# Two transformer blocks with 64 experts on one core: expert loops with sixteen blocks per turn, and the last output pass by column halves

## The chip, the core and the metric

The kernel runs on one core of a Trainium2 chip. The metric is the time of one execution on the device, in microseconds. Runs of the kernel before are 1090.98 to 1095.73 us, with a median of 1094.42 of three.

## The reference

256 tokens of 1024 features go through two layers. The first has three kinds of attention (block-wise, dilated, sliding window with sinks) with gated branches and an output projection. The second has a modulation by a condition, a short convolution beside a sparse attention, and then a mixture of experts. Only the last matters here:

```python
def moe(h, w_router, router_bias, w1, w3, w2, ws1, ws3, ws2):
    scores = sigmoid(t @ w_router)
    _, eidx = top_k(scores + router_bias, 8)              # 8 of 64 experts for each token
    g = take(scores, eidx); g = g / sum(g) * 2.5
    # (token, expert) pairs are sorted by expert and padded to blocks of 128 rows
    out = for each block: swiglu(t[toks], w1[e], w3[e], w2[e]) * gs[:, None]
    routed = segment_sum(out, row_tok)
    shared = swiglu(t, ws1, ws3, ws2)
    return routed + shared
x = x + gate2 * moe(h2, ...)
```

An expert has 1024 x 256 weights twice and 256 x 1024 once, 3 MB in float32. How many blocks have work depends on the data: at least one for each expert in use, at most 79. With these inputs there are 33.

## The kernel before

Each of the five engines has its own instruction stream, and semaphores join them. Up to about 685 us of the span the streams are straight: an order that the program works out while it is built. Then comes the expert part, where the number of blocks `n_work` is known only at run time. Each engine there has a `Fori` loop. A turn of it holds four blocks written one after the other (`BODY = 4`), since buffers rotate over four or two places and semaphore names hang on the block's number modulo 4. A turn is inside an `If` on the whole turn, and each block in it inside an `If` of its own. The number of turns is fixed when the program is built, for the most blocks that can be: 20 on each engine (19 on SP, whose first four blocks stand ahead). Where there are fewer blocks, the engine goes through the turns that are left and does nothing in them.

One block of TensorE (`expert_block`, L2018 to L2047) is 24 up matmuls (L2020, weights and rows each split into a rounded part and a rest, three products), the turning of the next block's gathered rows (L1997), the put of the block before into the four sum banks (`scatter`, L2005, four matmuls for each half of the columns), the turning of the hidden rows (L2035), the search for the tokens of the block after next (L1987), and 12 down matmuls (L2047). The first block stands apart ahead of the loop, so the loop holds blocks 1 to 78, 1 to 32 with these data.

One block of VectorE (L1643 to L1665) is the rests of the down weights (L1646), the rests of the next up weights (L1619), the product of the two hidden halves (L1651), the rests of the next rows (L1613), the rest of the hidden rows (L1654), two small ones on tokens and gates (L1605, L1606), more up weights, and `y_lo` for each half of the columns (L1663). ScalarE makes the rounded parts beside it. VectorE has no block apart. SP loads the weights of a block when the place is free (`down_lo`), GpSimd makes the pick and put matrices and gathers rows.

The end: after the loop TensorE runs 22 matmuls of ones into an unused bank (`keep_busy(("last_put",))`), then the put of the last block, eight matmuls over both halves of the columns and both groups of 128 tokens, and a one-column matmul that tells VectorE (`experts_summed`). VectorE multiplies each of four pieces of 128 x 512 by the gate (L1672) and adds it to `x` (L1675), and SP stores 128 tokens of 1024 columns when two pieces are there (L785):

```python
            for t in range(NT):
                sp.wait_ge(S("out_ready"), 2 * t + 2)
                sp.dma_start(out[0, t * P:(t + 1) * P, :], x[:, t, :]).then_inc(S("out_stored"), 16)
```

## Time and profile before

| What | us |
|---|---|
| median of three runs | 1094.42 |
| lowest and highest run | 1090.98, 1095.73 |
| the profiled execution, its own time | 1096.29 |
| its span, first to last instruction | 1094.5 |
| TensorE busy in the span | 1032.3 |
| VectorE busy in the span | 796.3 |
| ScalarE busy in the span | 585.7 |
| GpSimd busy in the span | 219.9 |

Busy time is the sum of an engine's instructions; branches, register and semaphore instructions are not counted. "Idle before" names what released an engine; "issue" is time in which it waited for nothing that the profile shows. The clock is that granted to TensorE, as a share of its full speed. The queues named "instruction" carry the program itself. The profiled execution is 1.8 us longer than its span and 1.9 us longer than the median.

### The profile page before, as it was taken

To read this page: it belongs to the slowest core of one execution; us is meant where nothing else is said; L and a number is where in the kernel's file an instruction comes from. 1 tells how busy PE (TensorE), PEld (TensorE's weight loads), DVE (VectorE), ACT (ScalarE), POOL (GpSimd) and SP (SyncE) were. 2 spreads that over 40 slices of the span, in tenths; PEclk is the share of its full clock that TensorE was granted. 3 is DMA by queue.
4 is the path that set the end of the run, shared out by engine and by line. 5 is a ranking of instruction groups with operands and counts; after the bars stand their busy time and mean duration, and the time that the engine had idled before them with its cause. 6 is when DMAs were issued, how large, how long until landed. Compare 5 with 4: busy or idle time off the path is not lost. (4 is left out here: it accounts for less than half of the span.)

```text
span 1094.5 us, 16677 instructions
## 1 busy us (share of the span) xinstructions
PE 1032.3 (94%) x5226; PEld 834.4 (76%) x5226; DVE 796.3 (73%) x1324; ACT 585.7 (54%) x895; POOL 219.9 (20%) x237
## 2 busy tenths in 40 slices
PE   8999999997999999998979899999999999999994
PEld 7778878786776676786769787778888888888883
DVE  4677887676754443556696554998999999999993
ACT  4455554433434332434344242777777777777771
POOL 4142220001000000041130001332423323323320
PEclk9999999998999899998999899999999999999998
DMA  9876766748525243435233215988888888888871
GB/s 317 276 266 220 268 237 212 233 163 284 193 96 173 92 154 116 165 94 214 89 107 126 77 59 210 348 304 326 338 310 331 341 306 335 334 309 344 333 287 57
DMA packets 91206, 247.40 MB, mean 226 GB/s; under 512 B 13244, under 2 KB 23925, under 8 KB 77842
## 3 DMA queue, kind: packets, MB, share of 16 engines
q1 hardware_dynamic: 84578, 226.36, 57.6%
q0 software_dynamic: 6000, 19.96, 4.8%
q8 instruction: 29, 0.48, 0.2%
q10 hardware_dynamic: 576, 0.41, 0.1%
q14 instruction: 23, 0.19, 0.0%
HBM read 244.27 MB, written 2.29 MB: 225 GB/s over the span
## 5 line engine op out<-in xcount | busy, mean ns | idle before, releaser
L1766 PE MATMUL bank<-w_hi,a_hi 128*128 128x512 f32 (+2 forms) x512 | 208.1, 406 | 11.2 <-DVE w_lo L1229 5.5
L1766 PE MATMUL bank<-w_lo,a_hi 128*128 128x512 f32 (+2 forms) x512 | 198.8, 388 | 0.0
L1766 PE MATMUL bank<-w_hi,a_lo 128*128 128x512 f32 (+2 forms) x512 | 198.7, 388 | 0.0
L1229 DVE TENSOR_TENSOR w_lo<-ring,w_hi 128x1024 fp32r<-128x1024 f32 (+2 forms) x134 | 154.7, 1179 | 51.2 <-ACT w_hi L952 46.8
L952 ACT ACTIVATE w_hi<-ring 128x1024 fp32r<-128x1024 f32 (+2 forms) x140 | 141.4, 1024 | 89.2 <-PE bank L1766 85.8
L1619 DVE TENSOR_TENSOR up_lo<-raw_weights,up_hi 128x1024 fp32r<-128x1024 f32 x136 | 164.2, 1248 | 3.0
L1112 ACT ACTIVATE up_hi<-raw_weights 128x1024 fp32r<-128x1024 f32 x136 | 135.8, 1050 | 0.0
L1766 PEld LDWEIGHTS bank<-w_hi,a_hi 128*128 128x128 f32 x512 | 98.0, 191 | 42.1 <-issue 20.1
L798 POOL TENSOR_SCALAR mean_squares<-mean_squares 128x8 f32<-128x8 f32 (+2 forms) x32 | 9.7, 302 | 549.8 <-ACT logits L905 294.7
L1766 PEld LDWEIGHTS bank<-w_hi,a_lo 128*128 128x128 f32 x512 | 98.1, 192 | 20.3
L1766 PEld LDWEIGHTS bank<-w_lo,a_hi 128*128 128x128 f32 x512 | 98.3, 192 | 18.6 <-issue 1.4
L2020 PE MATMUL bank<-up_hi,x_block_hi 128*128 128x512 f32 x264 | 104.3, 395 | 1.2 <-issue 1.2
L2020 PE MATMUL bank<-up_hi,x_block_lo 128*128 128x512 f32 x264 | 104.5, 396 | 0.0
L2020 PE MATMUL bank<-up_lo,x_block_hi 128*128 128x512 f32 x264 | 104.3, 395 | 0.0
L892 POOL TENSOR_SCALAR put<-block_rows,consts 128x256 fp32r<-128x256 f32 x33 | 39.7, 1203 | 242.4 <-PE bank L2005 128.1
L1646 DVE TENSOR_TENSOR down_lo<-raw_weights,down_hi 128x1024 fp32r<-128x1024 f32 x66 | 78.6, 1231 | 7.0 <-ACT down_hi L1129 7.0
L1382 DVE SCALAR_TENSOR_TENSOR ada_acc<-merged,c_col,ada_acc 128x512 f32<-128x512 f32 x84 | 62.8, 748 | 19.4 <-DMA merged<-in_w_ada_dram 16.7
L1129 ACT ACTIVATE down_hi<-raw_weights 128x1024 fp32r<-128x1024 f32 x66 | 66.0, 1050 | 0.3 <-issue 0.3
L1148 ACT ACTIVATE y_hi<-bank,block_gates 128x512 fp32r<-128x512 f32 x66 | 45.5, 689 | 31.3 <-PE bank L2047 31.3
L2020 PEld LDWEIGHTS bank<-up_hi,x_block_hi 128*128 128x128 f32 x264 | 49.6, 188 | 13.2 <-issue 1.4
L2020 PEld LDWEIGHTS bank<-up_lo,x_block_hi 128*128 128x128 f32 x264 | 49.6, 188 | 11.9
L2020 PEld LDWEIGHTS bank<-up_hi,x_block_lo 128*128 128x128 f32 x264 | 49.6, 188 | 11.8
(260 smaller groups left out, 1906.9 us busy)
## 6 DMA issues: line engine op xcount, KB each, us to landing
raw_weights<-in_w_dram SPq DMA_DIRECT2D x102, 1024.0 KB, 7.0
ring<-in_w_in_dram SPq DMA_DIRECT2D x58, 1024.0 KB, 5.3
merged<-in_w_ada_dram SPq DMA_DIRECT2D x96, 256.0 KB, 5.3
ring<-in_w_out_dram SPq DMA_DIRECT2D x8, 1024.0 KB, 5.4
ring<-in_w_branch_dram SPq DMA_DIRECT2D x6, 1024.0 KB, 5.0
bias<-rel_rows SPq DMA_DIRECT2D x40, 128.0 KB, 5.1
block_rows<-place_rows SPq DMA_DIRECT2D x34, 128.0 KB, 8.7
ring<-in_ws_dram SPq DMA_DIRECT2D x2, 1024.0 KB, 5.3
```

What stands on the lines that cost most here:

```text
L798: gp.tensor_scalar(msum[:, z, 0:width], msum[:, z, 0:width], 1.0 / count, EPS, ALU.mult, ALU.add)\
L892: gp.tensor_scalar(put[:, :], row4[:, r, :], consts[:, C_COL:C_COL + 1], None, ALU.is_equal)\
L952: act.activation(w_parts[0][:, 2 * p:2 * p + 2, 0:w], view(j, kind)[:, 2 * p:2 * p + 2, :], ACT.Copy)\
L1112: act.activation(up_hi[:, r % 2, 4 * kh:4 * kh + 4, m, :], raw_up(raw[:, 1 - r % 2, :], kh, m), ACT.Copy)\
L1129: act.activation(down_hi[:, f, :], raw[:, 1 - r % 2][:, UP + f * DM:UP + (f + 1) * DM], ACT.Copy)\
L1148: act.activation(y_hi[:, hf * CH:(hf + 1) * CH], y_b[hf][:, :], ACT.Copy, scale=gcol[:, r, 0:1])\
L1229: dve.tensor_tensor(w_parts[1][:, 2 * p:2 * p + 2, 0:w], view(JOB[it[1:3]], kind)[:, 2 * p:2 * p + 2, :], w_parts[0][:, 2 * p:2 * p + 2, 0 ...
L1382: dve.scalar_tensor_tensor(out=o, in0=ada_row(q), scalar=c_col[:, 1, k:k + 1], in1=o, op0=ALU.mult, op1=ALU.add) .then_inc(S("ada_step" if ...
L1619: dve.tensor_tensor(up_lo[:, r % 2, 4 * kh:4 * kh + 4, m, :], raw_up(raw[:, 1 - r % 2, :], kh, m), up_hi[:, r % 2, 4 * kh:4 * kh + 4, m, : ...
L1646: dve.tensor_tensor(down_lo[:, f, :], raw[:, 1 - r % 2][:, UP + f * DM:UP + (f + 1) * DM], down_hi[:, f, :].bitcast(F32), ALU.subtract).th ...
L1766: mm = pe.matmul(ps[:, 0:wide], a_parts[za][:, k, t * P:(t + 1) * P], w_parts[zw][:, k, 0:wide], start=start, stop=stop)
L2020: mm = pe.matmul(hidden_b[:, :], (xe_hi, xe_lo)[zx][:, k, :], (up_hi, up_lo)[zw][:, r % 2, k].rearrange("p m n -> p (m n)"), start=(k == 0 ...
```

## The change

`LONG` is 16. The loops of TensorE and VectorE get sixteen blocks in a turn, so 5 turns on each; the block's body stays as it was, and is a function on VectorE now. VectorE's first block stands ahead of its loop, as TensorE's did. The loops of ScalarE, GpSimd and SP are not changed. The 22 matmuls of ones and the one-column matmul are removed, and the last put of each half of the columns tells VectorE itself. VectorE works by halves: the two products of a half, then its two sums; SP stores each of the four pieces by itself.

```diff
--- before.py
+++ after.py
@@ -372,9 +372,10 @@
 KEEP_BUSY = {("start",): 16, ("half", "proj", 2, 0): 9, ("proj", 2, 0): 4, ("flip", 15, 2): 5,
              ("turn_branch", 2): 6, ("xturn", 1, 0): 4, ("xturn", 1, 1): 15, ("proj2", 0, 0): 4, ("turn2", 0, 3, 0): 7,
              ("turn2", 1): 10, ("value", 31): 8, ("turn_branch", 3, 1): 17, ("out2", 0, 0): 4, ("route", 0): 4,
-             ("route", 1): 5, ("ranks",): 7, ("tokens", 0): 5, ("last_put",): 22}
+             ("route", 1): 5, ("ranks",): 7, ("tokens", 0): 5}
 
 BODY = 4
+LONG = 4 * BODY
 UP, DOWN = 2 * KT * ED, FT * DM
 N_SMALL = 15
 N_LATE = 6
@@ -780,10 +781,12 @@
                         sp.wait_ge(S("down_lo"), 2 * i - 2)
                         load_down(r, load_up(i, r))
                         load_places(i, r)
-            for t in range(NT):
-                sp.wait_ge(S("out_ready"), 2 * t + 2)
-                sp.dma_start(out[0, t * P:(t + 1) * P, :], x[:, t, :]).then_inc(S("out_stored"), 16)
-            sp.wait_ge(S("out_stored"), 16 * NT)
+            for hf in range(2):
+                c = slice(hf * CH, hf * CH + CH)
+                for t in range(NT):
+                    sp.wait_ge(S("out_ready"), 2 * hf + t + 1)
+                    sp.dma_start(out[0, t * P:(t + 1) * P, c], x[:, t, c]).then_inc(S("out_stored"), 16)
+            sp.wait_ge(S("out_stored"), 16 * 2 * NT)
 
 
         @block.gpsimd
@@ -1636,43 +1639,50 @@
             rest_of_rows(0)
             dve.wait_ge(S("work_ready"), 2)
             n_work = dve.value_load(work[0:1, 0:1], min_val=0, max_val=MAX_WORK)
-            with dve.Fori(0, -(-MAX_WORK // BODY)) as m4, dve.If(n_work > m4 * BODY):
-                for r in range(BODY):
-                    i = m4 * BODY + r
+            def expert_block(i, r):
+
+                nxt = (r + 1) % BODY
+                for f in range(FT):
+                    dve.wait_ge(S("down_hi"), 2 * i + f + 1)
+                    dve.tensor_tensor(down_lo[:, f, :], raw[:, 1 - r % 2][:, UP + f * DM:UP + (f + 1) * DM],
+                                      down_hi[:, f, :].bitcast(F32), ALU.subtract).then_inc(S("down_lo"), 1)
+                for m in range(2):
+                    rest_of_up_weights(i + 1, nxt, 0, m)
+                dve.wait_ge(S("silu_done"), i + 1)
+                dve.tensor_tensor(he, hs[:, 0, :], hidden_b[:, ED:2 * ED], ALU.mult).then_inc(S("h_done"), 1)
+                rest_of_rows(i + 1)
+                dve.wait_ge(S("h_hi_ready"), i + 1)
+                dve.tensor_tensor(h_lo[:, :, :], turned_b[:, 0:ED].rearrange("p (f n) -> p f n", f=FT),
+                                  h_hi[:, :, :].bitcast(F32), ALU.subtract).then_inc(S("h_lo_ready"), 1)
+                take_tokens(i + 2, (r + 2) % BODY)
+                for m in range(2):
+                    rest_of_up_weights(i + 1, nxt, 1, m)
+                for hf in range(2):
+
+                    dve.wait_ge(S(f"y_hi_{hf}"), i + 1)
+                    c = slice(hf * CH, (hf + 1) * CH)
+                    dve.scalar_tensor_tensor(out=y_lo[:, c], in0=y_b[hf][:, :], scalar=gcol[:, r, 0:1],
+                                             in1=y_hi[:, c].bitcast(F32), op0=ALU.mult, op1=ALU.subtract)\
+                       .then_inc(S(f"y_lo_{hf}"), 1)
+
+            expert_block(0, 0)
+            with dve.Fori(0, -(-(MAX_WORK - 1) // LONG)) as turn, dve.If(n_work > turn * LONG + 1):
+                for b in range(LONG):
+                    i = turn * LONG + (b + 1)
                     with dve.If(n_work > i):
-                        nxt = (r + 1) % BODY
-                        for f in range(FT):
-                            dve.wait_ge(S("down_hi"), 2 * i + f + 1)
-                            dve.tensor_tensor(down_lo[:, f, :], raw[:, 1 - r % 2][:, UP + f * DM:UP + (f + 1) * DM],
-                                              down_hi[:, f, :].bitcast(F32), ALU.subtract).then_inc(S("down_lo"), 1)
-                        for m in range(2):
-                            rest_of_up_weights(i + 1, nxt, 0, m)
-                        dve.wait_ge(S("silu_done"), i + 1)
-                        dve.tensor_tensor(he, hs[:, 0, :], hidden_b[:, ED:2 * ED], ALU.mult).then_inc(S("h_done"), 1)
-                        rest_of_rows(i + 1)
-                        dve.wait_ge(S("h_hi_ready"), i + 1)
-                        dve.tensor_tensor(h_lo[:, :, :], turned_b[:, 0:ED].rearrange("p (f n) -> p f n", f=FT),
-                                          h_hi[:, :, :].bitcast(F32), ALU.subtract).then_inc(S("h_lo_ready"), 1)
-                        take_tokens(i + 2, (r + 2) % BODY)
-                        for m in range(2):
-                            rest_of_up_weights(i + 1, nxt, 1, m)
-                        for hf in range(2):
-
-                            dve.wait_ge(S(f"y_hi_{hf}"), i + 1)
-                            c = slice(hf * CH, (hf + 1) * CH)
-                            dve.scalar_tensor_tensor(out=y_lo[:, c], in0=y_b[hf][:, :], scalar=gcol[:, r, 0:1],
-                                                     in1=y_hi[:, c].bitcast(F32), op0=ALU.mult, op1=ALU.subtract)\
-                               .then_inc(S(f"y_lo_{hf}"), 1)
-
-            dve.wait_ge(S("experts_summed"), 1)
-            for t in range(NT):
-                for hf in range(2):
-                    tmp = qn[:, hf, :]
-                    o = x[:, t, hf * CH:hf * CH + CH]
-                    dve.tensor_tensor(tmp, acc_b[2 * t + hf][:, :], gate_bc[:, 1, hf * CH:hf * CH + CH], ALU.mult)\
+                        expert_block(i, (b + 1) % BODY)
+
+            for hf in range(2):
+                c = slice(hf * CH, hf * CH + CH)
+                dve.wait_ge(S("experts_summed"), hf + 1)
+                for t in range(NT):
+                    if hf:
+                        dve.wait_ge(S("out_ready"), t + 1)
+                    dve.tensor_tensor(qn[:, t, :], acc_b[2 * t + hf][:, :], gate_bc[:, 1, c], ALU.mult)\
                        .then_inc(S("final_step"), 1)
-                    dve.wait_ge(S("final_step"), 2 * t + hf + 1)
-                    dve.tensor_tensor(o, o, tmp, ALU.add).then_inc(S("out_ready"), 1)
+                for t in range(NT):
+                    dve.wait_ge(S("final_step"), 2 * hf + t + 1)
+                    dve.tensor_tensor(x[:, t, c], x[:, t, c], qn[:, t, :], ALU.add).then_inc(S("out_ready"), 1)
 
 
         @block.tensor
@@ -2071,18 +2081,14 @@
             mm.then_inc(S("block_done"), 1)
             turn_rows(0, 1)
             expert_block(0, 0, 1)
-            with pe.Fori(0, -(-(MAX_WORK - 1) // BODY)) as m4, pe.If(n_work > m4 * BODY + 1):
-                for b in range(BODY):
-                    i = m4 * BODY + (b + 1)
+            with pe.Fori(0, -(-(MAX_WORK - 1) // LONG)) as turn, pe.If(n_work > turn * LONG + 1):
+                for b in range(LONG):
+                    i = turn * LONG + (b + 1)
                     with pe.If(n_work > i):
-                        expert_block(i, (b + 1) % BODY, m4 + 1 + (b + 2) // BODY)
-            keep_busy(("last_put",), turned_b)
+                        expert_block(i, (b + 1) % BODY, turn * (LONG // BODY) + (1 + (b + 2) // BODY))
             pe.wait_ge(S("put_ready"), n_work)
             for hf in range(2):
-                mm = scatter(hf, n_work)
-            mm.then_inc(S("block_done"), 1)
-
-            pe.matmul(y_b[0][0:1, 0:1], ones[:, 0:1], ones[:, 0:1], start=True, stop=True).then_inc(S("experts_summed"), 1)
+                scatter(hf, n_work).then_inc(S("experts_summed"), 1)
 
 
 
```

In the built program, TensorE's stream behind the last block of its loop, before (`bank` stands for the sum banks and the unused one, `ones` for the filling):

```order
L2074 COMPARE_AND_BRANCH
L1706 MATMUL bank<-ones 128x128 x22
L2005 MATMUL bank<-y_hi,put 128x512 [waits y_lo_0,put_ready]
L2005 MATMUL bank<-y_lo,put 128x512
L2005 MATMUL bank<-y_hi,put 128x512
L2005 MATMUL bank<-y_lo,put 128x512
L2005 MATMUL bank<-y_hi,put 128x512 [waits y_lo_1]
L2005 MATMUL bank<-y_lo,put 128x512
L2005 MATMUL bank<-y_hi,put 128x512
L2005 MATMUL bank<-y_lo,put 128x512
L2085 MATMUL bank<-ones 1x1
L389 UNCONDITIONAL_BRANCH
```

and now:

```order
L2084 COMPARE_AND_BRANCH
L2015 MATMUL bank<-y_hi,put 128x512 [waits y_lo_0,put_ready]
L2015 MATMUL bank<-y_lo,put 128x512
L2015 MATMUL bank<-y_hi,put 128x512
L2015 MATMUL bank<-y_lo,put 128x512
L2015 MATMUL bank<-y_hi,put 128x512 [waits y_lo_1]
L2015 MATMUL bank<-y_lo,put 128x512
L2015 MATMUL bank<-y_hi,put 128x512
L2015 MATMUL bank<-y_lo,put 128x512
L390 UNCONDITIONAL_BRANCH
```

The filling matmuls and the one-column matmul between the loop and VectorE are gone, and the eight puts follow the loop's branch.

VectorE's stream behind its loop, before (`qn` is the temporary, L1672 the product with the gate, L1675 the sum):

```order
L1639 COMPARE_AND_BRANCH
L1672 TENSOR_TENSOR qn<-bank,gate_bc 128x512 [waits experts_summed]
L1675 TENSOR_TENSOR x<-x,qn 128x512 [waits final_step]
L1672 TENSOR_TENSOR qn<-bank,gate_bc 128x512
L1675 TENSOR_TENSOR x<-x,qn 128x512 [waits final_step]
L1672 TENSOR_TENSOR qn<-bank,gate_bc 128x512
L1675 TENSOR_TENSOR x<-x,qn 128x512 [waits final_step]
L1672 TENSOR_TENSOR qn<-bank,gate_bc 128x512
L1675 TENSOR_TENSOR x<-x,qn 128x512 [waits final_step]
L389 UNCONDITIONAL_BRANCH
```

and now (L1681 the product, L1685 the sum):

```order
L1669 COMPARE_AND_BRANCH
L1681 TENSOR_TENSOR qn<-bank,gate_bc 128x512 [waits experts_summed]
L1681 TENSOR_TENSOR qn<-bank,gate_bc 128x512
L1685 TENSOR_TENSOR x<-x,qn 128x512 [waits final_step] x2
L1681 TENSOR_TENSOR qn<-bank,gate_bc 128x512 [waits out_ready,experts_summed]
L1681 TENSOR_TENSOR qn<-bank,gate_bc 128x512 [waits out_ready]
L1685 TENSOR_TENSOR x<-x,qn 128x512 [waits final_step] x2
L390 UNCONDITIONAL_BRANCH
```

Products and sums alternated behind one signal; now two products stand ahead of two sums, once for each half.

## Rows read from the trace of the kernel before

**Rows 1.** The page: busy time, share of the span and instructions of each engine.
```profile
PE 1032.3 (94%) x5226; PEld 834.4 (76%) x5226; DVE 796.3 (73%) x1324; ACT 585.7 (54%) x895; POOL 219.9 (20%) x237
```

**Rows 2.** Stretches, one per TensorE turn: us, busy time of each engine, clock, DMA.
```profile
697.25:744.87 47.62, 46.67 (x226) 38.09 (x224) 43.56 (x58) 35.77 (x48) 17.89 (x18) 1.00 0.85 322
...
977.68:1024.02 46.34, 46.34 (x225) 38.04 (x224) 43.29 (x58) 35.73 (x48) 15.25 (x17) 1.00 0.87 330
```

**Rows 3.** Waits of TensorE, 697.25 to 1070.8: us in total, times, longest.
```profile
PE bank L1997 <- DMA x_gathered<-h_rows,block_tokens: 1.1, 3, 0.5
```

**Rows 4.** Chain that ended last: start us, us, what.
```profile
1021.30 2.88 PE bank L2047 x12
1024.18 5.59 PE bank L2020 x24
...
1032.99 2.89 PE bank L2047 x12
1035.88 5.60 PE bank L2020 x24
...
1070.71 6.27 issue
```

**Rows 5.** Timeline of TensorE: start us, us, instruction, idle before it.
```profile
1066.39 0.39 PE L2035 MATMUL bank<-consts,hT 128*128 128x128 f32 x2
...
1070.08 0.62 PE L2047 MATMUL bank<-down_hi,h_lo 128*128 128x512 f32 x2
1076.98 7.02 PE L1706 MATMUL bank<-ones 128*128 128x128 f32 x44 [6.27 <-issue]
1083.75 0.47 PE L2005 MATMUL bank<-y_hi,put 128*128 128x512 f32 x1
...
1085.78 0.19 PE L2085 MATMUL bank<-ones 128*1 128x1 f32 x2
```

**Rows 6.** Timeline of VectorE over the last block and the end.
```profile
1060.73 2.42 DVE L1646 TENSOR_TENSOR down_lo<-raw_weights,down_hi 128x1024 fp32r<-128x1024 f32 x2 [0.23 <-ACT down_hi L1129]
...
1065.35 0.41 DVE L1651 TENSOR_TENSOR hT<-hs,bank 128x256 f32<-128x256 f32 x1
...
1071.46 0.75 DVE L1663 SCALAR_TENSOR_TENSOR y_lo<-bank,block_gates,y_hi 128x512 fp32r<-128x512 f32 x1 [0.21 <-ACT y_hi L1148]
1086.01 0.69 DVE L1672 TENSOR_TENSOR qn<-bank,gate_bc 128x512 f32<-128x512 f32 x1 [13.79 <-PE bank L2085]
...
1090.71 0.69 DVE L1675 TENSOR_TENSOR x<-x,qn 128x512 f32<-128x512 f32 x1
```

**Rows 7.** Stretches behind the last down matmul; columns as in rows 2.
```profile
1070.80:1073.90 3.10, 0.00 (x0) 0.00 (x0) 1.20 (x2) 0.63 (x1) 0.00 (x0) 1.00 0.59 169
1074.10:1080.60 6.50, 3.62 (x17) 3.63 (x18) 0.00 (x0) 0.00 (x0) 0.00 (x0) 0.50 0.00 0
1081.00:1083.70 2.70, 2.70 (x26) 2.70 (x26) 0.00 (x0) 0.00 (x0) 0.00 (x0) 1.00 0.00 0
```

**Rows 8.** Line L785, SP's stores: ns min/median/max to issue one.
```profile
L785 SPq DMA_DIRECT2D out_dram<-x x2: 343/355/367, 1088.8 to 1091.4; - x2
```

**Rows 9.** DMA issues, whole span: KB each, median us to landing.
```profile
out_dram<-x SPq DMA_DIRECT2D x2, 512.0 KB, 2.6
...
block_rows<-place_rows SPq DMA_DIRECT2D x34, 128.0 KB, 8.7
...
place_rows<-prow SPq DMA_DIRECT2D x1, 128.0 KB, 1.7
```

**Rows 10.** DMA queues, 742 to 744, the instruction queue: packets, MB, share.
```profile
q14 instruction: 1, 0.01, 1.0%
```

**Rows 11.** DMA queues, 745 to 1071, all there are.
```profile
q1 hardware_dynamic: 19851, 89.60, 72.4%
q0 software_dynamic: 4032, 14.68, 11.2%
```

**Rows 12.** DMA queues, 734 to 736, the other instruction queue.
```profile
q8 instruction: 1, 0.02, 3.3%
```

## The prediction

> **What bounds the kernel now.** I read four views in this order: the page's busy times, the stretches by turn of the expert loop, the chain that ended last, and the timeline after the last block.
>
> TensorE is busy 94% of the span, VectorE 73% [rows 1]. In the expert loop TensorE has no slack: eight turns of four blocks take 46.3 to 47.6 us, of which it works 46.3 to 46.7 [rows 2], 11.6 us a block. VectorE works 43.2 to 43.6 us of the same stretches, so it is nearly full too, with some 0.8 us free per block. All that TensorE waits for in these 373 us is the gathered rows, 1.1 us [rows 3]. Going from one turn to the next is not seen: the chain has the down matmuls ending at 1024.18 and the next up matmuls starting there, where a turn of TensorE ends, just as at 1035.88 inside a turn [rows 4].
>
> The end is different. The last down matmul ends at 1070.71; TensorE then does nothing for 6.27 us, with "issue" as its reason, runs the 44 pieces of its 22 filling matmuls for 7.02 us, and only at 1083.75 starts the last puts, although VectorE had finished what they need at 1072.21 [rows 5, 6]. The 6.27 us stand where the loop goes through its empty turns: it is written for up to 79 blocks, 33 are there, and the eight turns of work are followed by twelve in which the outer test fails, 0.52 us each. After the puts come eight VectorE operations, 1086.01 to 1091.40, and 3.1 us until the span ends.
>
> **The change part by part.**
>
> *Empty turns on TensorE.* The loop has 5 turns, 2 in use and 3 empty. At 0.52 us they cost 1.57 in place of 6.27: the puts can start at 1072.28, just behind VectorE's 1072.21. I take 0.52 although TensorE's sequencer may have run ahead of the matmuls, which would make a turn a little dearer and start it a little earlier; both ways the end stays near 1072. The Trainium skill, in Advanced Engine Details and Errata, Control Flow Timing, gives 108 ns for a compare-and-branch, and an empty turn has two. By that, twelve would take 2.6 us and nine fewer would save 1.9 us. The trace has 6.27 us for them, so the trace's price stands.
>
> *Filling matmuls.* They go: minus 7.02 us [rows 5]. They were there for the clock. It is at 1.00 until 1073.9 and at 0.50 from 1074.1 to 1080.6 [rows 7]: it fell some 3.3 us after TensorE stopped. If TensorE stops for 0.7 to 3 us only, the puts run at 1.00. At 0.50 a piece of filling takes 0.20 us instead of 0.10 (3.63 us for 18, 2.70 for 26), so the four puts ahead of VectorE would cost 0.9 us more. I take nothing and keep 0.9 for the range.
>
> *Signals by half.* The last matmul of each column half now tells VectorE, so it starts after four puts, not eight and the one-column matmul. Before, 1083.75 to 1086.01 is 2.26 us; now 4 x 0.233 and the delay of some 0.3 make 1.25: minus 1.0.
>
> *Sums and stores.* VectorE's eight operations are the same in shape and number, reordered: two products, two sums, per half. At 5.39 us for eight [rows 6] they cost the same. The new waits on `out_ready` protect the temporary; they name an operation at least two before, so nothing is added. The second half's signal comes 0.93 us after the first, inside the first four operations. SP now issues four stores instead of two, 0.36 us each [rows 8], and the last starts behind the last sum as before. It carries 256 KB instead of 512: two of 512 KB took 2.6 us to land [rows 9], with the data part about half of it, so minus 0.6.
>
> *Sum if nothing else happens:* the puts start at 1072.28, VectorE at 1073.5, ends at 1078.9, and 2.5 us later, at 1081.4, the span ends: minus 13.1.
>
> *Fewer back edges.* TensorE has one between blocks in place of seven, VectorE one (after block 16) in place of eight. By the chain each is worth nothing while the code is at hand [rows 4].
>
> *Longer loops.* This is where I see a cost. A block is 56 matmuls with as many weight loads and some 13 other instructions; the loop's body on TensorE grows from about 500 to 2000 instructions, on VectorE from 100 to 400. Before, the last instruction packet is on the wire between 742 and 744 [rows 10]; from 745 to 1071 only the two data queues move anything [rows 11]. So the whole short loop stayed at hand. Whether the long one does, no row shows. If it does not, the way back needs a fetch. Its price from below: one 16 KB packet takes 3.3% of 2 us of 16 engines, 1.1 us [rows 12]; a small transfer in a quiet stretch, the 128 KB of `place_rows`, lands after 1.7 us, and the stores after 2.6. From above: 128 KB under the loop's load take 8.7 us [rows 9], but those stand behind megabytes in their own queue, and instructions have a queue of their own. I take 3 us inside the loop and 2 to 2.6 at the end, nearer to the packet and the quiet transfers, and keep 1.1 and 8.7 for the range.
>
> In the middle, VectorE's fetch starts when its last y_lo is under way: 0.75 us of that, the 0.2 us it waits for `down_hi` anyway, and the 0.6 us between its product for the hidden rows (done 1065.76) and the transpose of it (1066.39) [rows 5, 6] hide 1.6 of the 3. TensorE loses 1.4 us, and its own fetch lies behind the queued down matmuls and beside that: 1.5 in all. At the end VectorE's loop leaves after 1072.2 + 2.3 + 3 x 0.52 = 1076.1; it starts 2.6 us later than in the sum above. TensorE's own 2.3 us put its start at 1074.6 and its first half at 1075.8, ahead of that. So 13.1 - 1.5 - 2.6 = 9.0 us are left.
>
> **Which of the two?** The Trainium skill, in Runtime: NRT & Kernel Launch, Instruction fetch mechanics, says that a taken branch to a target outside a window of two pages forces a fetch before execution goes on. With it already the short loop of TensorE, 500 instructions long, would fetch on its jumps, and the trace shows none [rows 11]. The page also has 2048 instructions for TensorE and 512 for the others; by that the long bodies fit barely, if what is fetched ahead pushes nothing out. My choice is a judgement: what keeps 500 instructions at hand need not keep 2000, and on VectorE 400 need not stay where 100 did; that one of the two has lost its head by the end of a turn is a little likelier than not.
>
> **The rivals.**
>
> *A. Everything stays at hand.* Then the sum above: minus 13.1, 1081.3. For it: the short loop kept all of its code. Against it: nothing of this length has been tried in the trace. 32%.
>
> *B. One fetch, but under load at the price of loaded transfers [rows 9].* VectorE's way back after block 16 waits up to 8.7 us, 7.1 of them seen by TensorE: 13.1 - 7.1 - 2.6 = 3.4 saved, 1091.0. Against it: an instruction packet has its own queue. 8%.
>
> *C. Every jump between the loop's head and its end fetches.* The three empty turns on VectorE then cost two fetches each: its last operations start at 1072.2 + 6p + 1.57, and with the middle p - 1.6 the span ends at 1080.1 + 7p. At p = 2 that is 1094.1, no change; it is slower than before by over 0.5% from p = 2.9 on, 1101 at 3. For it: head and end are 2000 instructions apart. Against it: once head and end have both been fetched, nothing in an empty turn needs a third place. 8%.
>
> *D. The turns never were the 6.27 us,* and TensorE waited for something unseen. Then that idle time stays, the filling matmuls go, and 13.1 - 4.7 = 8.4 are saved, 1086.0. Against it: all that the puts need was there at 1072.21. 4%, and it lies in the forecast's range.
>
> **How the numbers follow.** The profiled execution took 1096.29 us with a span of 1094.5; the median of the runs is 1094.42, and the savings are taken off that. The forecast (one fetch on each way back) has 48%: 1094.4 - 9.0 = 1085.4, by itself 1083 to 1089. The range reaches down to A with its own spread, and up to a dearer fetch: 1080.5 to 1090. It leaves out most of B and C. A measurement tells 0.5%, 5.5 us, from no change: faster is below 1088.9, slower above 1099.9. Faster: the forecast's 46, A's 32, D's 4 and a little of B, 0.85; slower: C above 2.9 us a fetch, 0.05; the rest, 0.10, is within.
>
> **What would show it.** In the changed profile: no filling matmuls after the last down matmul; TensorE idle there for 1.5 us (A) or 3.5 to 4.5 (forecast); VectorE's first final product within 1.3 us of the first put (A) or held up 1 to 2 us more by its own loop; instruction packets on their queues still at the end of the span and around block 16 to 17 (forecast), none there (A), several among the empty turns (C). Around block 17 one stretch of TensorE longer by 1 to 2 us. The puts at clock 1.00, 0.23 us apart. The eight last operations in 5.4 us. I am wrong if the gap after the last down matmul stays at 6 us, if the loop's 373 us grow by over 4, or if the end after VectorE's last sum is not shorter.

## The result, and the profile after

The changed kernel is slower: 1105.18 us median (1099.62 to 1107.52), the kernel before 1093.43 (1090.98 to 1095.73), ratio 1.0092 with a 95% interval of 1.0068 to 1.0117. The profiled execution took 1099.62 us with a span of 1097.8, so it is the quickest of its runs; its span is 3.3 us longer than the 1094.5 of before. The accounts below are of the two profiled executions, and most of the 11.75 us between the medians is not in them (see "what stays open").

The 3.3 us of span are the sum of a loop that lost and an end that gained. From the start of the second block to the start of the last, before took 361.6 us (697.25 to 1058.83), the changed kernel 374.75 (697.17 to 1071.92): +13.2. From the last down matmul to the end, before took 23.8 us (1070.71 to 1094.5), now 14.2 (1083.64 to 1097.8): -9.6. The start and the last block together give -0.3.

**The loop.** The waits of TensorE from the second block to the last down matmul (us in total, times, longest), where [rows 3] had 1.1 us, 3 times:

```profile
PE bank L2007 <- DMA x_gathered<-h_rows,block_tokens: 6.8, 11, 1.2
PE bank L2030 <- issue: 4.1, 1, 4.1
```

The second line is the one way back. It stands in the timeline of TensorE between block 16 and block 17 (start, us, instruction, idle before it):

```profile
887.72 0.63 PE L2057 MATMUL bank<-down_hi,h_lo 128*128 128x512 f32 x2
892.41 0.49 PE L2030 MATMUL bank<-up_hi,x_block_hi 128*128 128x512 f32 x1 [4.07 <-issue]
...
893.36 0.63 PE L2030 MATMUL bank<-up_hi,x_block_hi 128*128 128x512 f32 x1
893.78 0.63 PE L2030 MATMUL bank<-up_lo,x_block_hi 128*128 128x512 f32 x1
...
896.34 0.44 PE L2030 MATMUL bank<-up_lo,x_block_hi 128*128 128x512 f32 x1
896.62 0.40 PE L2030 MATMUL bank<-up_hi,x_block_lo 128*128 128x512 f32 x1
```

and in that of VectorE, at its own way back:

```profile
895.10 2.36 DVE L1647 TENSOR_TENSOR down_lo<-raw_weights,down_hi 128x1024 fp32r<-128x1024 f32 x2 [5.24 <-issue]
```

The idle 4.07 us are not all of TensorE's fetch. The duration of its jumps (PEldq is the sequencer that feeds TensorE; count, ns min/median/max, first and last start) gives it whole:

```profile
L2084 PEldq COMPARE_BRANCH  x2: 75/3120/6165, 885.5 to 891.9; - x2
```

The sequencer runs ahead of the matmuls. It took the jump back at 885.5 and held it for 6.17 us, and the down matmuls already issued kept TensorE busy for the first 2.9 of them, until 888.35. The rest and a few instructions ahead of the first matmul are the 4.07. One packet of q14, at 892.8, lies in VectorE's idle time; the next, at 895.4, came when VectorE was at work again.

After the 4.07 us the matmuls stand 0.43 us apart instead of 0.23 until 896.3: the clock had dropped. The windows show it (columns as in [rows 2]): the granted clock is 1.00 during the rest and 0.50, its lower level, once TensorE is back.

```profile
888.40:892.30 3.90, 0.00 (x0) 0.00 (x0) 1.25 (x2) 3.90 (x5) 0.91 (x2) 1.00 0.98 381
...
893.30:896.30 3.00, 3.00 (x8) 2.34 (x7) 1.20 (x2) 0.00 (x0) 0.00 (x0) 0.50 0.07 22
```

Block 16 with the way back took 15.78 us, block 17 13.21, against some 11.6: 5.8 us for one turn.

The rest of the 13.2 us are the late gathers. Outside those two blocks, 11 blocks took more than 12.1 us, 8.8 us over 11.6 in all; before, two did (12.18 and 12.32). What is new in the profile is the instruction queues. From 745 on, before had only data queues moving [rows 11]; the changed kernel, 697 to 1058:

```profile
q8 instruction: 15, 0.25, 0.3%
q14 instruction: 10, 0.08, 0.1%
```

q8 brings 16 KB at a time to TensorE (experiments 6 and 7 tell the queues apart), one packet for about every second block: eight for a turn of sixteen. Their times here are to 0.5 us. Apart from those of the way back, 14 packets of q8 lie in the loop. Each of the 11 long blocks had one on the wire while its gathered rows were: the rows are asked for 1.6 us before the block starts and needed 5.6 us after, and the packets were at 710.5, 734.5, 758.5, 784, 817.5, 839.5, 865, 908.5, 931.5, 955.5 and 1060, with those blocks starting at 708.7, 732.7, 756.5, 780.2, 816.3, 840.2, 864.1, 905.6, 929.5, 953.3 and 1059.5. No block without one was over 12.1 us. The landings say the same. In the changed kernel the gathers that were issued 10.0 to 10.3 us into a block, with a packet of q8 starting 1 to 4 us behind the issue, took 7.7 to 7.9 us to land (seven of them; an eighth, with two packets in its flight at the way back, took 8.8). Before, the twenty issued 10.0 to 10.5 us into a block with no packet took 6.5 to 7.4, with a median of 6.95.

**The end.** TensorE, in place of [rows 5]:

```profile
1083.01 0.63 PE L2057 MATMUL bank<-down_hi,h_lo 128*128 128x512 f32 x2
1088.10 0.77 PE L2015 MATMUL bank<-y_hi,put 128*128 128x512 f32 x1 [4.46 <-issue]
1088.66 0.63 PE L2015 MATMUL bank<-y_lo,put 128*128 128x512 f32 x1
1089.09 0.63 PE L2015 MATMUL bank<-y_hi,put 128*128 128x512 f32 x1
```

VectorE, in place of [rows 6]:

```profile
1084.40 0.75 DVE L1664 SCALAR_TENSOR_TENSOR y_lo<-bank,block_gates,y_hi 128x512 fp32r<-128x512 f32 x1 [0.21 <-ACT y_hi L1151]
1090.37 1.29 DVE L1681 TENSOR_TENSOR qn<-bank,gate_bc 128x512 f32<-128x512 f32 x2 [5.22 <-PE bank L2015]
1091.58 1.28 DVE L1685 TENSOR_TENSOR x<-x,qn 128x512 f32<-128x512 f32 x2
```

The 5.22 us are put down to the puts, but the chain that ended last goes through VectorE's own jumps (DVEq is its sequencer; start, us, what):

```profile
1084.48 0.06 DVEq L1669
1084.55 3.68 issue
1088.22 0.06 DVEq L1669
...
1088.39 0.28 issue
1088.68 0.04 DVEq L1669
...
1088.81 0.23 issue
1089.04 0.06 DVEq L1669
...
1090.37 1.29 DVE qn L1681 x2
```

That is one fetch of 3.68 us and then six pairs of records some 0.4 us apart, two for a turn: three empty turns of 0.7 us. TensorE's jumps at the end:

```profile
L2084 PEldq COMPARE_BRANCH  x7: 83/221/4902, 1080.8 to 1087.8; - x7
```

Its fetch took 4.90 us from 1080.8, 2.9 of them behind the last down matmuls, and three empty turns of some 0.7 us followed. The instruction queues, 1081 to 1097.8, move again:

```profile
q8 instruction: 3, 0.05, 1.5%
q14 instruction: 3, 0.02, 0.5%
```

### The profile page after: what moved, and what is told of

Same layout as the page of the kernel before. It is cut to its first block and busy times, and to the rows that moved or that the text cites. A ratio compares the mean times of both kernels' runs of the same rounds, so it can differ in the third digit from the quotient of the medians.

```text
span 1097.8 us, 16465 instructions
## 1 busy us (share of the span) xinstructions
PE 1028.8 (94%) x5180; PEld 829.0 (76%) x5180; DVE 795.7 (72%) x1324; ACT 585.6 (53%) x895; POOL 219.4 (20%) x237
## 5 line engine op out<-in xcount | busy, mean ns | idle before, releaser
L2015 PE MATMUL bank<-y_hi,put 128*128 128x512 f32 x132 | 58.4, 442 | 4.5 <-issue 4.5
```

Of the source, the lines that this page charges most:

```text
L2015: mm = pe.matmul(acc_b[2 * t + hf][:, :], put[:, t * P:(t + 1) * P], part[:, hf * CH:hf * CH + CH], start=False, stop=False, skip_group_ch ...
```

## The experiments

The diffs are against the changed kernel where nothing else is said. Beside each stand the median, its ratio to the kernel before on the same chip with the interval, and "the loop", start of the second block to start of the last in the profiled execution (before 361.6, changed 374.75).

**1. The new end alone** (loops of four blocks as before).

```diff
-LONG = 4 * BODY
+LONG = BODY
 # VectorE: the loop of before, Fori(0, -(-MAX_WORK // BODY)), expert_block(i, r) inside
```

> Loops of four as before (VectorE's first block inside its loop), only the end of the kernel changed: no filling matmuls, signals by half, sums and stores by half. Theory F (long loop bodies do not stay in the instruction memory; their fetches cost at each way back, and each 16 KB instruction packet that is on the wire while rows are gathered delays the gather, for which TensorE waits): blocks of 11.6 us as before, no instruction packet after 745, twelve empty turns of 6.3 us, puts from about 1077.0 but at the low clock, 0.43 us each, span about 1086, 8 less than before. Rival R (the new end loses, by four stores or by reordered sums, and the loops gain): the end after the last down matmul is not shorter than before's 23.8 us, span 1094 or more.

1088.75 us, 0.9940 [0.9920, 0.9959]; loop 360.75. The first final product of VectorE:

```profile
1076.55 1.29 DVE L1680 TENSOR_TENSOR qn<-bank,gate_bc 128x512 f32<-128x512 f32 x2 [8.05 <-issue]
```

Its y_lo had ended at 1068.49. VectorE has eleven empty turns here, at 0.71 us each, and they end after TensorE's (first put 1073.36, after 6.38 us of issue). So VectorE's empty turns had been there all along, behind the filling matmuls. The trace of the kernel before has them too, at its own loop:

```profile
L1639 DVEq COMPARE_BRANCH  x23: 56/59/66, 1072.4 to 1080.2; - x23
```

**2. The long loops alone** (the filling matmuls and the end of before put back).

```diff
+            keep_busy(("last_put",), turned_b)
...
-                scatter(hf, n_work).then_inc(S("experts_summed"), 1)
+                mm = scatter(hf, n_work)
+            mm.then_inc(S("block_done"), 1)
+
+            pe.matmul(y_b[0][0:1, 0:1], ones[:, 0:1], ones[:, 0:1], start=True, stop=True).then_inc(S("experts_summed"), 1)
...
```

VectorE's last operations and SP's stores are those of before too.

> Loops of sixteen and VectorE's first block apart as in the change, but the old end with its filling matmuls. Theory F: the expert loop loses as in the change, some 13 us from the second to the last block (about 6 of it around the sixteenth block, the rest by gathers), the idle time after the last down matmul falls from 6.3 to 4.5, span about 1105, 11 more than before. Rival R: the loops gain or lose nothing, span 1090 to 1095.

1108.55 us, 1.0131 [1.0096, 1.0165]; loop 375.09. The loss is the long loops', with the way back at 15.77 and 13.21 us as in the changed kernel, and 14 waits for gathered rows, 7.7 us in all (11 and 6.8 there).

**3. Eight blocks per turn.**

```diff
-LONG = 4 * BODY
+LONG = 2 * BODY
```

> The change with eight blocks in a turn instead of sixteen. TensorE's body is 1000 instructions, VectorE's 200. Theory F: packets go on through the first turn alone, until about 800, and TensorE's late gathers with them; no stall at the ways back (blocks 8, 16, 24); six empty turns of about 0.5 us; span 1084 to 1087. Rival S (one page of TensorE's code is all that stays, or VectorE's block apart is what hurts): stalls of 4 us at each of three ways back or late gathers in every turn, span 1097 or more.

1086.75 us, 0.9909 [0.9888, 0.9931]; loop 364.2. Instruction packets run until 784, once through the body, and none follow; the ways back cost nothing. The four blocks of 12.3 to 13.2 us are the ones those packets fall in (blocks 2, 4, 6 and 8); from block 9 on none is over 12.0.

**4. The gather issued ahead of the put on GpSimd,** with sixteen blocks per turn.

```diff
+                        gather_rows(i + 2, after)
...
-                        gather_rows(i + 2, after)
```

The call now stands ahead of the wait for `block_done` and of the put.

> The change as it is, but GpSimd issues the gather of rows ahead of making the put matrix instead of behind it, so the gather starts 0.4 to 0.5 us earlier, and 1.5 to 2 us in the blocks in which the put matrix takes 1.97 us. Theory F: the instruction packets stay as they are, about one each 25 us on TensorE's queue, but the late gathers shrink from 0.8 to 0.3 us or nothing; the loop from the second to the last block gets some 5 us shorter than the change's 374.7, the two ways back stay at 4 us; span about 1092. Rival: the slow blocks are slow for another reason than the gather: nothing moves by over 1 us.

1105.65 us, 1.0096 [1.0068, 1.0123]; loop 374.5. The expectation failed: in most blocks the gather starts at 9.91 us into the block instead of 9.99, because it waits for its indices, which come from TensorE and VectorE in the same block. Only in every fourth block did the new order help, 9.9 in place of 11.3. The loop lost what the changed kernel's did, with 11 waits for gathered rows, 6.6 us. (The profiled execution, 1094.54 us, is by far the quickest of its five; its loop is no shorter for that, but its first expert block starts at 681.9 us where the changed kernel's starts at 686.5.)

**5. Sixteen blocks per outer turn, but code for four** (an inner loop of four turns of four blocks).

```diff
             with pe.Fori(0, -(-(MAX_WORK - 1) // LONG)) as turn, pe.If(n_work > turn * LONG + 1):
-                for b in range(LONG):
-                    i = turn * LONG + (b + 1)
+                with pe.Fori(0, LONG // BODY) as m4, pe.If(n_work > turn * LONG + m4 * BODY + 1):
+                    for b in range(BODY):
+                        i = turn * LONG + m4 * BODY + (b + 1)
...
```

The same is done on VectorE.

> The change with its sixteen blocks per turn written as an inner loop of four turns of four blocks (TensorE and VectorE, the first block apart, the new end). The number of empty outer turns is the change's, three, but the code that is gone through is 500 instructions on TensorE and 100 on VectorE. Theory F: no instruction packets after about 745, no stall around block 16, late gathers in the first four blocks only, from the second to the last block some 362 us; VectorE's way out costs three empty turns of 0.7 us after its last y_lo; span 1081 to 1083, some 12 less than before. Rival (what hurts is the data-dependent leaving of turns, or VectorE's block apart, not the length of the code): as the change, 1097 or more.

**1083.03 us**, 0.9892 [0.9852, 0.9931]; loop 360.7. This keeps what the change gained and loses none of it: waits of TensorE in the loop, and its first put,

```profile
PE bank L2008 <- DMA x_gathered<-h_rows,block_tokens: 1.1, 3, 0.6
```

```profile
1068.01 0.62 PE L2058 MATMUL bank<-down_hi,h_lo 128*128 128x512 f32 x2
1069.33 0.47 PE L2016 MATMUL bank<-y_hi,put 128*128 128x512 f32 x1 [0.69 <-DVE y_lo L1664]
```

The put now waits for y_lo and for nothing else. The instruction queues move as little as before, 697 to 1058:

```profile
q8 instruction: 2, 0.03, 0.0%
q14 instruction: 3, 0.02, 0.0%
```

**6 and 7. The long body on one engine only.**

In 6 VectorE has the loop of before:

```diff
-            with dve.Fori(0, -(-(MAX_WORK - 1) // LONG)) as turn, dve.If(n_work > turn * LONG + 1):
+            with dve.Fori(0, -(-MAX_WORK // BODY)) as m4, dve.If(n_work > m4 * BODY):
...
```

and in 7 VectorE keeps sixteen blocks and TensorE has `BODY` in the place of `LONG`:

```diff
-            with pe.Fori(0, -(-(MAX_WORK - 1) // LONG)) as turn, pe.If(n_work > turn * LONG + 1):
+            with pe.Fori(0, -(-(MAX_WORK - 1) // BODY)) as turn, pe.If(n_work > turn * BODY + 1):
...
```

> Sixteen per turn on TensorE alone; VectorE as before in fours, with its first block inside; the new end. Theory F: the 16 KB packets go on through the span, and with each of them a gather 0.5 to 0.9 us late; one stall of about 4 us on TensorE after block 16, with the clock lowered behind it; VectorE's eleven empty turns of 0.7 us end 8 us after its last y_lo. Loop from the second to the last block 372 to 375 us, span about 1096 to 1099.

1105.07 us, 1.0100 [1.0067, 1.0134]; loop 375.3, 16 packets of q8 in it as in the changed kernel, a way back of 15.91 and 14.34 us, 6.8 us of waits for gathered rows. TensorE's body alone makes the whole loss of the loop.

> Sixteen per turn on VectorE alone, its first block apart; TensorE in fours; the new end. Theory F: only 8 KB packets go on, one per five blocks or so, and late gathers are rare; after block 16 VectorE stands for about 5 us, and TensorE loses some 4 us with it; the end waits for TensorE's twelve empty turns, 6.3 us. Loop from the second to the last block 365 to 368 us, span 1088 to 1091.

1094.92 us, 1.0001 [0.9984, 1.0017]; loop 367.2. There are 10 packets of q14 and only 2 of q8, and blocks are late as seldom as before; the 6 us come from one place, VectorE's way back:

```profile
892.36 2.36 DVE L1647 TENSOR_TENSOR down_lo<-raw_weights,down_hi 128x1024 fp32r<-128x1024 f32 x2 [5.40 <-issue]
```

TensorE waits 3.5 us for `hT` then, its clock drops, and the block takes 17.90 us. With both long (the changed kernel) the two fetches lie beside each other, and the turn costs 5.8, not their sum. The packets of q14, 8 KB each, that fell in a gather's flight here (762, 820, 954.5, 1012.5) went with blocks of 11.55 to 11.7 us. That does not clear them: all four came in the last 0.1 to 0.8 us of the flight, where those of q8 that went with late blocks came 1 to 5 us behind the issue.

**8. Thirty-two per outer turn, code for four.** As 5 with `LONG = 8 * BODY`.

> As e5_nested_16, with eight inner turns, so 32 blocks to an outer turn, three outer turns, one in use and two empty. Theory F: the same loop as e5, and one empty turn less on VectorE's way out, but four more inner steps never run empty with 33 blocks: 0.7 us below e5_nested_16, which is within the noise of the runs. Rival: as e5.

1083.13 us, 0.9888 [0.9854, 0.9921]; loop 361.3. VectorE idles 0.73 us ahead of its first product in place of the 1.28 of 5, which the medians don't tell apart: there is next to nothing left to gain from fewer empty turns.

**9. Twelve blocks per turn.** As 3 with `LONG = 3 * BODY`.

> The change with twelve blocks in a turn: 1500 instructions in TensorE's loop, 300 in VectorE's, three turns in use (the last with eight blocks), four empty. It asks how long a body stays. Theory F with about 2000 instructions of room on TensorE and about 500 on VectorE, and the next packets fetched ahead: both still stay; packets until about 835 and six late gathers in the first turn, no stall after blocks 12 and 24; loop from the second to the last block about 366 us, VectorE's way out 0.7 us for each empty turn; span about 1085. If the room is smaller: packets through the whole span, stalls of 4 to 5 us after blocks 12 and 24, a loop of 378 us or more, span about 1100.

1086.32 us, 0.9920 [0.9895, 0.9944]; loop 363.5. Packets of q8 at 710.5, 734, 758, 788, 816.5 and 838.5, then none:

```profile
q8 instruction: 6, 0.10, 0.1%
```

No way back is seen. The body is some 1500 instructions on TensorE and 300 on VectorE and stays at hand; some 2000 and 400 do not. The late blocks end with the packets, but for one of 12.04 us.

**10. The loop counts made exact** on the kernel of 1: 8 turns on TensorE and 9 on VectorE, which covers these inputs only and leaves out the blocks beyond the 33rd that other inputs could need.

```diff
-            with pe.Fori(0, -(-(MAX_WORK - 1) // LONG)) as turn, pe.If(n_work > turn * LONG + 1):
+            with pe.Fori(0, 8) as turn, pe.If(n_work > turn * LONG + 1):
...
-            with dve.Fori(0, -(-MAX_WORK // BODY)) as m4, dve.If(n_work > m4 * BODY):
+            with dve.Fori(0, 9) as m4, dve.If(n_work > m4 * BODY):
```

> e1_tail_alone with the numbers of turns cut to those that these inputs use (eight on TensorE, nine on VectorE), which serves 33 blocks and no others: the work for more than 36 blocks is left out. Theory F: without empty turns the idle time of 6.4 us on TensorE and 8.0 us on VectorE goes, the puts run at full clock, VectorE's first product comes 1.2 us after the first put; span 6 to 7 us below e1_tail_alone at the same start, 1077 to 1079, as e5_nested_16. Rival (the idle time behind the last block is something else than empty turns): it stays at 6 us, span 1084.

1083.32 us, 0.9882 [0.9847, 0.9917]. TensorE's idle time ahead of the puts is 0.69 us in place of 6.38, VectorE's 0.39 in place of 8.05. So both were the empty turns, twelve on TensorE and eleven on VectorE; what one costs is in the next section. With them gone the first product comes 1.20 us after the first put (1071.25, 1072.45), as forecast for the signals by half (1.25).

**11 and 12. Transfers put into the gathers' flight,** on the kernel of 5.

Of 11, with a 16 in the place of the two ones that give the rows in 12:

```diff
+        side_dst = nc.dram_tensor("side_dst", (1, 4096), F32, kind="Internal").ap()
...
+                        if r % 2 == 1:
+                            act.wait_ge(S("side"), 16 * (2 * m4 + (1 + r // 2)))
+                            act.dma_start(side_dst, bass.AP(a["ws2_2"].tensor, 0, [[4096, 1], [1, 4096]])).then_inc(S("side"), 16)
```

It stands behind ScalarE's second y_hi of every second block. One more transfer stands ahead of ScalarE's loop, and a wait for the last one behind it.

> The nested version of e5 with nothing changed in its code, but ScalarE issues a transfer of 16 KB, the size of one of TensorE's instruction packets, in every second block (17 in all), right behind its last y_hi, so that it lies in the flight of the gathered rows, as the instruction packets of the long bodies do. It goes from one place of device memory to another and nobody reads it (the computed result is the full one). Theory that the packets themselves hold up the gathers: if it goes over the wire as one or a few large packets, most of the 15 blocks concerned in the stretch from the second to the last block grow by 0.4 to 0.8 us, the stretch from 360.7 to 367-372, the median from 1083 to about 1089-1095, and TensorE's wait for x_gathered from 1.1 us to 5-8. If it is cut into small packets over all 16 DMA engines, each engine gets a sixteenth and it costs nearly nothing; then the run with 256 KB decides. Rival, that the gathers are late for another reason that goes with the long bodies (GpSimd's start, the jumps): 360.7 and 1083 as in e5, wait 1.1.

1084.22 us, 0.9901 [0.9875, 0.9926]; loop 365.2. The 16 KB went in 32 packets of 512 bytes, small pieces as in the case named in the expectation. By its median it can't be told from 5; the profiled execution, with the longer loop, is the slowest of its four (1088.86 us).

> The same as e11 with 256 KB in each of the 17 transfers, 16 rows of 16 KB, so that every DMA engine has about 16 KB more to move in the flight of every second gather: what one instruction packet does to one engine, done to all. Theory that a gather is as late as its most loaded DMA engine: each of the 15 blocks grows by 0.5 to 1 us, the stretch from 360.7 to 368-376, the median to 1090-1099. Rival, that 16 KB on an engine does not hold up the gather: 360.7 and 1083, or at most the share of bandwidth: 4 MB more at 330 GB/s is 13 us of wire time over the whole loop, of which nothing shows while TensorE is the bound.

1095.95 us, 1.0014 [0.9999, 1.0029]; loop 373.5, 12.8 us more than 5, or 0.85 for each of the 15 transfers in it. What it added, and what TensorE waited for, 697 to 1060:

```profile
q10 hardware_dynamic: 480, 3.93, 2.9%
```

```profile
PE bank L2014 <- DMA x_gathered<-h_rows,block_tokens: 10.9, 15, 1.4
```

Of the 15 blocks whose gather met a transfer 13 took 12.2 to 13.2 us; of the others one did (12.3), and the rest took 11.55 to 11.9. So 256 KB more at that moment, 16 KB for each of the 16 DMA engines if its 32 packets of 8 KB spread evenly, are enough to make a gather 0.85 us late, the size of the 0.8 us of the long blocks. With the instruction queues as quiet as before, it also shows that the code need not be long for this. It does not show that the most loaded engine decides: at the loop's 320 to 330 GB/s [rows 2] 256 KB are 0.8 us of all engines together, so a rule that goes by the sum of the load gives the same price.

## Why the prediction was wrong

The forecast was 1085.4 us with a range of 1080.5 to 1090; 1105.18 is above the range and in the part called slower (above 1099.9), which had 5%, all of it for rival C. The sign that the prediction had named came: its 373 us of the loop, to the last down matmul, grew by 13.0.

**"I take 3 us inside the loop": the place was right, the price too low.** Both engines fetched at their way back, as forecast, once between block 16 and 17. But VectorE stood for 5.24 us there, and TensorE's jump took 6.17 and left it idle for 4.07, where each fetch stood at 3. The same fetches took 3.68 and 4.90 us at the end, when the DMA engines were 0.43 busy (1083.7 to 1088) and not 0.98; no run varies the load by itself. The two lie side by side, as assumed. To that comes the clock, which I had in hand only for the end: after the rest of 4.07 us TensorE ran at 0.50 for some 3 us. The turn cost 5.8 us where 1.5 stood.

**"It keeps its code or fetches it at the way back": the step that failed.** I saw an instruction packet only as something an engine waits for. Every one of the eight packets per turn comes again in the second turn, and in the first turn eight come instead of two. Apart from the way back TensorE waits for none of these; they are fetched ahead. But they share the DMA engines with the gathered rows, the one transfer of the loop that TensorE waits for at all: asked for at 10 us into the block and needed 7.2 us later, for a landing of 6.8. That [rows 3] showed three waits on it at all should have told me that it stood at its limit. The late gathers cost 7.4 us, more than the turn, and none of the four cases had them. Forecast and actual differ by 12.3 us on the profiled executions (1096.3 - 9.0 = 1087.3 against 1099.6): 7.4 from the gathers, 4.3 from the turn (5.8 for 1.5), 0.9 from the end (9.6 saved for 10.5), less the 0.3 of the start and the last block.

**The end came out nearly right, in part by luck.** 10.5 of the 13.1 us were to be left there after the fetch, and 9.6 were. TensorE idled 4.46 us (forecast 3.5 to 4.5), but out of other terms: a fetch of 4.90 us where 2.3 stood, less the 2.9 that its queued matmuls hid, which the sum did not have, and 2.4 us of empty turns and first steps where 1.57 stood. VectorE's fetch took 3.68 where 2.3 stood, and its three empty turns 0.7 each where 0.52 stood; against that the eight last operations took 4.9 us and not 5.4. The 2.5 us from the last sum to the end were right. The filling matmuls, given as 7.02 us, hold the first put back by 6.77 (1076.98 to 1083.75); the sum of 13.1 goes by the start times and has it right. The "I take nothing" for the clock fell in its condition: TensorE stopped for 4.46 us, not 0.7 to 3, so most of the puts ran 0.43 us apart. The forecast's own start of the puts, 1074.6, was already 3.9 us after the last down matmul, beyond the 3.3 after which [rows 7] has the clock low. It cost nothing, since VectorE was later still. Experiment 5, which has the code at hand, reaches 1083.0 us (1080.1 to 1085.5), 11.8 us below before by its ratio, where rival A's sum was 13.1.

**"Fewer back edges" at nothing: right.** Loops of 360.7 us with a turn every 4 blocks (1, 5) say so.

**The empty turns at 0.52 us: wrong on both engines.** That figure is the 6.27 us of idle time spread over twelve turns. TensorE's jumps before the change say more:

```profile
L2074 PEldq COMPARE_BRANCH  x25: 82/210/216, 1067.8 to 1076.8; - x25
```

Those are two for each of the twelve turns and one that leaves, over 9.0 us: 0.75 us a turn. They begin 2.9 us before the last down matmul ends, so the first four turns or so cost nothing. The prediction had seen this possibility and called it harmless, and for three turns it was: their 1.57 us should have been nothing, and the first put waits only for the first half's y_lo, as experiment 5 shows with 0.69. For other numbers of turns it matters. With six (experiment 3) TensorE idles 1.90 us, where 0.52 us a turn would be 3.1. On VectorE a turn is 0.71, and before the change eleven of them ran behind the filling matmuls unseen; that is why the new end alone brings 7.4 us (1) and not the 12 of experiment 5. That the filling matmuls hid them too was missing from the prediction.

**Rival B** had the right kind of event in the middle, a fetch dearer than at the end, at 1091.0. **Rival C** fell: VectorE's three empty turns had one fetch, not six. **Rival D** fell with experiment 10. **Rival A** holds for bodies up to twelve blocks. The Trainium skill, in Runtime: NRT & Kernel Launch, Instruction fetch mechanics, gives 2048 instructions for TensorE and 512 for the others. As a forecast of what stays in a loop the runs do not bear these figures out: some 2000 and 400 were fetched anew each turn, 1500 and 300 stayed. Between them the place of the limit is not known, and 2000 is close enough to 2048 that only VectorE's 400 is well under its figure.

**What stays open.** Three things. The runs of the changed kernel reach from 1099.6 to 1107.5 us and the profiled one is the lowest, so 5.6 us between it and the median are in no trace here, and the profiled execution of before lies 2.9 above its median; with the 3.3 of the spans these make up the 11.75. 2 and 6 have the same wide spread (7.7 and 8.0 us) and 4 a wider one (14.8), 3, 8 and 9 stay within 3.1. Against experiment 5, which is this change with short code, the gap is better covered: 2.0% or some 22 us by the ratios, 18.7 by the spans. Which of the 16 DMA engines an instruction packet takes wasn't seen: 12 adds 32 packets at once, and that a single engine's 16 KB is enough was concluded from the coincidence of packets, late landings and late blocks in the changed kernel, 2, 3, 6 and 9, not tried by itself. For it speaks that the same 16 KB in 32 small packets (11) made next to no block late. And three packets of q8 in the changed kernel (987, 1006, 1034) went with blocks of only 11.6 to 11.9 us. Two of them had started 0.4 us before the gather was asked for, the third 0.5 us before it landed; that this is why they cost less was not tried.

## What to carry to other kernels

When a loop is unrolled, the code itself becomes traffic. Ask two things of the trace: whether instruction packets stop after the first turn, and which transfer has no slack while they run. Price an empty turn by the sequencer's jumps and not by the engine's idle time, since the sequencer may have started them while the engine was still busy. Where only the count of empty turns is too high, an inner loop around the short body (experiment 5, 1083.0 us, 1.1% below the kernel before) removes the turns without making the code longer.

## What was not expected of the hardware

- An empty turn of two tests costs 0.71 us on VectorE here and 0.75 on TensorE, whose first 2.9 us of turns are hidden behind matmuls already issued.
- The fetch at a jump took 6.17 us on TensorE in the loop and 4.90 at the end; VectorE stood 5.24 and 3.68 us.
- An instruction packet of 16 KB that nobody waits for went with a gather some 0.8 us late.
- Two products and then two sums of 128x512 on VectorE take 1.29 us as a pair, and the pairs start 1.20 us apart: the eight last operations took 4.9 us in pairs, where product and sum in turn, each sum waiting for its product, took 5.39.
- TensorE's clock was still at 1.00 (2.4 GHz) when it came back after 4.07 us of rest, and fell to 0.50 (1.2 GHz) only then, from 893.0 to 896.4: here the rest was paid for after it was over. At the end of the same kernel, after a rest of 4.46 us, it was not: the clock was at 1.00 until 1087.5 and at 0.50 from 1087.6, before the first put at 1088.10.
